# Filler matmuls on TensorE while a norm is computed, in a two-block transformer kernel on one core

## The chip, the cores and the metric

The kernel runs on one core of one Trainium2 chip. The metric is the device time of one execution in microseconds (us); three runs of the kernel before gave 3535.11, 3535.67 and 3539.28 us, median 3535.67. TensorE is PE in the rows (PEld is its loading of stationary operands), VectorE is DVE, ScalarE is ACT, GpSimd is POOL, SyncE is SP.

## The reference, cut to what matters

The input x is 512 tokens by 1024 features. A first block runs twice (l = 0, 1) and a second, hybrid block once. Each part begins with an RMS norm of x along the features:

```
x = x + 0.5*g1 * swiglu(modulate(x, sh1, sc1), ffn1_gate[l], ffn1_up[l], ffn1_down[l])
x = x + g2 * token_mix(modulate(x, sh2, sc2), ...)      # attention branches, gates, output projection
x = x + 0.5*g3 * swiglu(modulate(x, sh3, sc3), ffn2_gate[l], ffn2_up[l], ffn2_down[l])
modulate(x, shift, scale) = x * rsqrt(mean(x*x) + 1e-6) * (1 + scale) + shift
# after both l: rms_norm(x) * final_norm, then the hybrid block:
x = x + merged(rms_norm(x)*norm1_g) @ w_o               # four branches with gates
x = x + square(relu((rms_norm(x)*norm2_g) @ w_up)) @ w_down
```

shift, scale and the gates g come from c_act @ w_ada[l] + b_ada[l]. The next matmuls need the normed x, and the norm needs the whole updated x: at every such border TensorE has to wait.

## The kernel before, in words

x lies in SBUF transposed, as 8 tiles of 128 features x 512 tokens (f32). Weights stream from HBM in one fixed order (`plan()`) through five `raw` buffers. ScalarE rounds each block to fp32r (`wh`), VectorE takes the rest (`wl`), and TensorE multiplies three times per tile pair: `wh*uh + wl*uh + wh*ul` (`three()`, called by `fm()`, L445 to L447). `uh` and `ul` are the two parts of the normed x. Each engine's program is one Python function; they are ordered by semaphores counted in a dry pass. Nothing plans by cost: the order of calls is the order of instructions on each engine.

The stages, with the names used in keys: f10 (first feed-forward, l = 0), m0 (token mix), f20 (second feed-forward), then f11, m1, f21, then "s" (final norm and the hybrid block's first norm), the hybrid block's four branches, and "up" (its feed-forward).

A border works like this (m0 as the example). While the last output tiles are made, GpSimd adds the squares of x tiles 0 to 6 into `acc`; ScalarE squares tile 7 into `tmp1`. TensorE in `norm()` (L498) then does, in order: `sums()` of `acc` (four f32 matmuls with one column of ones, L488), a wait for `tmp1`, `sums()` of `tmp1`, and `row()` (L491 to L496): four f32 matmuls of 128x128, ones times a diagonal that holds 1/rms, which spreads 1/rms over all partitions. Between the sums and the row, VectorE adds the two means (L1471, L1476), GpSimd takes the power -1/2 (L2109) and VectorE builds the diagonal (L1467). After the row, VectorE scales tile k (L1500), ScalarE adds the shift and rounds (L980), VectorE makes `ul` (L1491), for k = 0 to 7. The first two weight blocks after a border are multiplied side by side (`fm_pair()`), six matmuls for each k as it comes.

At the beginning (f10) the squares of x are made by ScalarE and VectorE in `fsq`; TensorE waits for the constants (`CONST`, the tensor `cst` with `ones` and `ident` in it), then does 16 f32 sums (L900 and L901), then the row. The first weights are multiplied in `ffn(first=True)`, L521 to L523.

An f32 matmul stands as two instructions in the trace, and an fp32r one as one ("x8" is four f32 matmuls).

PSUM has eight banks `ps0` to `ps7`. `take(g, b=None)` (L417 to L430) gives a result its bank: the next of a ring when b is None, bank b otherwise. It makes TensorE wait until the bank's last owner was read, if that owner has a reader that frees it:

```
b = ring[0][ring[1] % len(ring[0])]; ring[1] += 1
last = in_bank.get(b); in_bank[b] = g
if last is not None:
    for s in (s_act, s_dve):
        if ("free", last) in s.at: pe.wait_ge(*s["free", last])
```

The ring holds all eight banks in the first block. After each attention its counter is set to 4 (L690). `second()`, the hybrid block, sets it to `[range(6), 0]`: it begins at bank 0 and leaves banks 6 and 7 to the gates; at its end it is set to `[range(8), 0]`. Before `second()`, the sums `("fs", 0)` to `("fs", 2)` and the rows `("r1",)` and `("r", "s")` take the next five banks. VectorE's `apply()` frees the bank of `("r", "s")` with its last tile, `frees=g if k == (0 if after_k else n - 1)` at L1500, since it reads the row out of PSUM for each of the eight tiles.

Of the kernel before, what the change touches and what calls it, by code (L numbers as in the profile page):

```python
# [243 lines left out]
def program(nc, A, OUT):  # L244
# [19 lines left out]
    def sb(ctx, name, shape, dt=F32):  # L264
        return ctx.enter_context(nc.sbuf_tensor(f"s_{name}", shape, dt))

    ps = [top.enter_context(nc.psum_tensor(f"ps{i}", [128, 512], F32)) for i in range(8)]
    cst = sb(top, "cst", [128, ncol])
    x = sb(top, "x", [128, 8, 512])
# [81 lines left out]
    def col(name, i=0, n=1):  # L351
        a, w = cols[name]
        assert i + n <= w
        return cst[:, a + i:a + i + n]

    sA, sB, yh, yl = mq, mk, uh, ul
    ident, ones = col("ident", 0, 128), col("ones", 0, 128)
# [33 lines left out]
    s_x_at = lambda k: (s_x[k // 2], 16)  # L391
# [21 lines left out]
    def tensor_engine(pe, TE):  # L413
# [4 lines left out]
        def take(g, b=None):  # L418
            if b is None:
                b = ring[0][ring[1] % len(ring[0])]  # L420
                ring[1] += 1
            last = in_bank.get(b)
            in_bank[b] = g
            bank_of[g] = b
            if last is not None:
                for s in (s_act, s_dve):
                    if ("free", last) in s.at:
                        pe.wait_ge(*s["free", last])
            return ps[b]
# [56 lines left out]
        def sums(o, at, ap):  # L486
            for b in range(4):
                ins = TE.matmul(o[:, at + b:at + b + 1], ap[:, sl(b)], ones[:, 0:1], start=True, stop=True)  # L488
            return ins

        def row(g, dg):  # L491
            o = take(g)
            for b in range(4):
                pe.wait_ge(*s_dve["diag", g, b])
                ins = TE.matmul(o[:, sl(b)], ones, dg[:, sl(b)], start=True, stop=True)  # L495
            ins.then_inc(*s_pe.up(("ps", g)))  # L496

        def norm(st, parts, dg):  # L498
            for j, (ap, wait) in enumerate(parts):
                o = take(("ms", st, j))  # L500
                pe.wait_ge(*wait)
                sums(o, 0, ap).then_inc(*s_pe.up(("ps", ("ms", st, j))))
            row(("r", st), dg)

        def ffn(st, first=False):
            _, g, u, d, nf = stages[st]
# [35 lines left out]
        def tail(st):  # L542
            return [(acc, s_pool["sq", st]), (tmp[1], s_act["tail", st])]
# [194 lines left out]
        def second():  # L738
# [155 lines left out]
            s_pe.mark(("end", "s"))  # L894
            ring[:] = [list(range(8)), 0]

        pe.wait_ge(*CONST)
        o = take(("ms", "f10", 0))
        for k in range(4):
            pe.wait_ge(*s_dve["sq0 pair", k])  # L900
            ins = sums(o, 4 * k, uf(2 * k + 1))  # L901
        ins.then_inc(*s_pe.up(("ps", ("ms", "f10", 0))))
        row(("r", "f10"), tmp[3])
        for l in range(2):
            if l:
                norm("f11", tail("f11"), tmp[2])
            ffn(f"f1{l}", l == 0)
            norm(f"m{l}", tail(f"m{l}"), tmp[2])
            mix(l)
            norm(f"f2{l}", tail(f"f2{l}"), tmp[2])  # L910
            ffn(f"f2{l}")
        o = take(("fs", 0))
# [4 lines left out]
        o = take(("fs", 1))  # L917
        pe.wait_ge(*s_act["tail", "s"])
        sums(o, 0, tmp[1]).then_inc(*s_pe.up(("ps", ("fs", 1))))
        o = take(("fs", 2))  # L920
# [1375 lines left out]
    for engine in (tensor_engine, scalar_engine, vector_engine, pool_engine, sync_engine):  # L2296
        engine(Waits(), Blank())
# [9 lines left out]
    @block.tensor  # L2307
    def _(e):
        tensor_engine(Waits(e), nc.tensor)
# [170 lines left out]
```

## Time and profile before

| | us |
|---|---|
| three runs, median | 3535.67 |
| three runs, lowest and highest | 3535.11, 3539.28 |
| profiled execution, its own time | 3532.56 |
| its span, first to last instruction | 3530.8 |
| PE busy | 3435.0 |
| mean granted TensorE clock | 0.983 |

The page of the profile gives busy time by engine; the other views used are the waits (who waited for whom), the timeline (start, duration, engine, line, operation, in brackets the idle time before and its releaser), and a table by stretches, which has the granted clock of each. A granted clock of 1.00 is 2.4 GHz, one of 0.50 is 1.2 GHz. In the first 28 us the record of the clock has no entry and shows 1.00; the durations of the matmuls tell it there.

### The profile page before, as it was taken

To read this page: it belongs to the slowest core of one execution; us is meant where nothing else is said; L and a number is where in the kernel's file an instruction comes from. 1 tells how busy PE (TensorE), PEld (TensorE's weight loads), DVE (VectorE), ACT (ScalarE), POOL (GpSimd) and SP (SyncE) were. 2 spreads that over 40 slices of the span, in tenths; PEclk is the share of its full clock that TensorE was granted. 3 is DMA by queue.
4 is the path that set the end of the run, shared out by engine and by line. 5 is a ranking of instruction groups with operands and counts; after the bars stand their busy time and mean duration, and the time that the engine had idled before them with its cause. 6 is when DMAs were issued, how large, how long until landed. Compare 5 with 4: busy or idle time off the path is not lost.

```text
span 3530.8 us, 40839 instructions
## 1 busy us (share of the span) xinstructions
PE 3435.0 (97%) x16646; PEld 2758.3 (78%) x16646; DVE 1786.8 (51%) x3100; ACT 1185.1 (34%) x1990; POOL 287.3 (8%) x238
## 2 busy tenths in 40 slices
PE   8999999999999999999899999999999999999999
PEld 6888786777888788887777878887788777878887
DVE  7666456565565733334654643334453655454433
ACT  3222236542222232223555332223321444223322
POOL 0000220002000200021200100013011000020000
PEclk9999999999999999999999999999999999999999
DMA  6565322123565523223210322322221223122232
GB/s 239 206 211 189 101 78 72 40 69 109 191 219 196 179 98 99 92 95 107 68 49 25 114 83 84 108 82 93 68 78 55 75 73 115 42 96 84 96 107 78
DMA packets 120218, 376.37 MB, mean 107 GB/s; under 512 B 13280, under 2 KB 28000, under 8 KB 120032
## 3 DMA queue, kind: packets, MB, share of 16 engines
q1 hardware_dynamic: 120032, 373.76, 31.8%
q8 instruction: 133, 2.18, 0.3%
q14 instruction: 53, 0.43, 0.0%
HBM read 371.61 MB, written 2.10 MB: 106 GB/s over the span
## 4 chain that ended last, share of the span: by engine, by line
PE 92%; DVE 4%; ACT 2%; issue 1%; POOL 1%; DMA 0%; SPq 0%; POOLq 0%; ACTq 0%; DVEq 0%
PE ps L445 26%; PE ps L446 26%; PE ps L447 26%; PE ps L660 2%; PE ps L683 2%; PE ps L554 2%; PE ps L488 1%; PE ps L495 1%; PE ps L479 1%; PE ps L481 1%; PE ps L480 1%; DVE s_wl L1429 1%; ACT s_wh L944 1%; POOL s_small L2109 0%; PE ps L521 0%
## 5 line engine op out<-in xcount | busy, mean ns | idle before, releaser
L445 PE MATMUL ps<-s_uh,s_wh 128*128 128x512 f32 x2824 | 1137.4, 403 | 30.2 <-DVE s_ul L1491 12.8
L1429 DVE TENSOR_TENSOR s_wl<-s_raw,s_wh 128x1024 fp32r<-128x1024 f32 (+3 forms) x645 | 707.1, 1097 | 845.2 <-ACT s_wh L944 843.0
L446 PE MATMUL ps<-s_uh,s_wl 128*128 128x512 f32 x2824 | 1111.1, 393 | 0.0
L447 PE MATMUL ps<-s_ul,s_wh 128*128 128x512 f32 x2824 | 1110.5, 393 | 0.0
L944 ACT ACTIVATE s_wh<-s_raw 128x1024 fp32r<-128x1024 f32 (+3 forms) x645 | 587.9, 913 | 727.6 <-PE ps L447 531.2
L445 PEld LDWEIGHTS ps<-s_uh,s_wh 128*128 128x128 f32 x2824 | 537.5, 190 | 173.1 <-issue 49.4
L447 PEld LDWEIGHTS ps<-s_ul,s_wh 128*128 128x128 f32 x2824 | 536.6, 190 | 115.1
L446 PEld LDWEIGHTS ps<-s_uh,s_wl 128*128 128x128 f32 x2824 | 537.9, 190 | 109.0 <-issue 2.4
L447 PE MATMUL ps<-s_fl,s_wh 128*128 128x512 f32 x960 | 378.2, 394 | 0.0
L445 PE MATMUL ps<-s_fh,s_wh 128*128 128x512 f32 x960 | 378.2, 394 | 0.0
L446 PE MATMUL ps<-s_fh,s_wl 128*128 128x512 f32 x960 | 378.2, 394 | 0.0
L447 PEld LDWEIGHTS ps<-s_fl,s_wh 128*128 128x128 f32 x960 | 179.5, 187 | 44.5
L446 PEld LDWEIGHTS ps<-s_fh,s_wl 128*128 128x128 f32 x960 | 179.5, 187 | 44.4
L445 PEld LDWEIGHTS ps<-s_fh,s_wh 128*128 128x128 f32 x960 | 179.5, 187 | 44.3
L1011 ACT ACTIVATE s_fh<-s_tmp 128x512 fp32r<-128x512 f32 x120 | 75.8, 632 | 407.3 <-DVE s_tmp L1537 382.4
L1005 ACT ACTIVATE s_tmp<-ps 128x512 f32<-128x512 f32 x120 | 71.7, 597 | 352.8 <-PE ps L447 348.4
L1438 DVE CUSTOM_DVE_ANT_0 s_raw<-s_raw,s_crow 128x1024 f32<-128x1024 f32 x144 | 181.3, 1259 | 0.7 <-DMA s_raw<-w 0.7
L1537 DVE TENSOR_TENSOR s_tmp<-s_tmp,ps 128x512 f32<-128x512 f32 x88 | 60.4, 687 | 178.0 <-PE ps L447 174.2
L2115 POOL TENSOR_TENSOR s_acc<-s_x 128x512 f32<-128x512 f32 x7 | 8.8, 1261 | 1608.1 <-DVE s_x L1519 1544.5
L1463 DVE TENSOR_TENSOR s_fl<-s_tmp,s_fh 128x512 fp32r<-128x512 f32 x120 | 83.1, 692 | 83.8 <-ACT s_fh L1011 83.8
L1519 DVE SCALAR_TENSOR_TENSOR s_x<-ps,s_mod,s_x 128x512 f32<-128x512 f32 x80 | 60.0, 750 | 105.0 <-PE ps L447 105.0
L1128 ACT ACTIVATE s_mT<-ps 128x128 f32<-128x128 f32 (+3 forms) x144 | 57.3, 431 | 145.4 <-PE ps L554 145.4
(401 smaller groups left out, 3374.1 us busy)
## 6 DMA issues: line engine op xcount, KB each, us to landing
s_raw<-w SPq DMA_DIRECT2D x616, 512.0 KB, 3.6
s_raw<-w SPq DMA_DIRECT2D x96, 192.0 KB, 2.4
s_raw<-w SPq DMA_DIRECT2D x64, 256.0 KB, 2.6
s_raw<-w SPq DMA_DIRECT2D x19, 128.0 KB, 2.0
s_x<-x SPq DMA_DIRECT2D x4, 512.0 KB, 6.3
out<-s_x SPq DMA_DIRECT2D x8, 256.0 KB, 2.2
s_raw<-w SPq DMA_DIRECT2D x4, 420.0 KB, 3.6
s_crow<-crow SPq DMA_DIRECT2D x2, 512.0 KB, 3.4
```

What stands on the lines that cost most here:

```text
L445: TE.matmul(o, w_hi(i, k), h, start=first, stop=False)
L446: TE.matmul(o, w_lo(i, k), h, start=False, stop=False)
L447: return TE.matmul(o, w_hi(i, k), l, start=False, stop=last)
L554: ins = TE.transpose(o[:, sl(j)], p[:, sl(j)], ident)
L660: TE.matmul(o[g][:, 0:L], q, k, start=True, stop=True).then_inc(*s_pe.up(("ps", ("S", (st, 2 * t + g)))))
L683: ins = TE.matmul(o[g], v, mT[(n + g) % 4][:, sl(j)], start=kind == "mla" and j == 0, stop=j == i and (kind == "mla" or br == 1))
L944: SC.activation(wh[slot[t]][:, 0:n], raw[t % NRAW][:, 0:n], ACT.Copy).then_inc(*s_hi.up(("hi", t)))
L1005: SC.activation(s[:], bank(("g", st, jj))[:], ACT.Silu if u else ACT.Relu).then_inc(*s_act.up(("gate", st, jj), frees=("g", st, jj)))
L1011: SC.activation(fh[:, j, :], s[:], ACT.Copy).then_inc(*s_act.up(("hh", st, jj)))
L1429: V.tensor_tensor(wl[w][:, 0:n], raw[t % NRAW][:, 0:n], wh[w][:, 0:n].bitcast(F32), SUB).then_inc(*s_lo.up(("lo", t)))
L1438: V.tensor_tensor_reduce(raw[i % NRAW][:], raw[i % NRAW][:], crow[:], 1.0, 0.0, MUL, ADD, mod[:, o:o + 1]).then_inc(*s_dve.up(("raw", i)))
L1463: V.tensor_tensor(dst, src, hi.bitcast(F32), SUB).then_inc(*s_dve.up(key))
```

## The change

A helper `keep_warm(o, n)` writes n f32 products of constants (ones times the first 512 columns of `cst`, 128x512) into a bank that nobody reads. `norm()` now first takes a bank for them, then puts one after the first sums, three after the last sums, and two after the row. It is called at six borders: m0, f20, f11, m1, f21 and up. The "s" border does not go through `norm()` and gets none. At the beginning, a bank is taken, four f32 products of x's tile 0 with itself run as soon as x's first part has landed, and three and two products of constants stand after the sums and after the row. Nothing reads these results; the output does not change.

```diff
+        def keep_warm(o, n):
+            for _ in range(n):
+                TE.matmul(o[:], ones, cst[:, 0:512], start=True, stop=True)
+
         def norm(st, parts, dg):
+            spare = take(("spare", st))
             for j, (ap, wait) in enumerate(parts):
                 o = take(("ms", st, j))
                 pe.wait_ge(*wait)
                 sums(o, 0, ap).then_inc(*s_pe.up(("ps", ("ms", st, j))))
+                keep_warm(spare, 3 if j else 1)
             row(("r", st), dg)
+            keep_warm(spare, 2)
...
+        spare = take(("spare", "f10"))
+        pe.wait_ge(*s_x_at(0))
+        for _ in range(4):
+            TE.matmul(spare[:], x[:, 0, 0:128], x[:, 0, :], start=True, stop=True)
         pe.wait_ge(*CONST)
         o = take(("ms", "f10", 0))
         for k in range(4):
             pe.wait_ge(*s_dve["sq0 pair", k])
             ins = sums(o, 4 * k, uf(2 * k + 1))
         ins.then_inc(*s_pe.up(("ps", ("ms", "f10", 0))))
+        keep_warm(spare, 3)
         row(("r", "f10"), tmp[3])
+        keep_warm(spare, 2)
```

## Rows read from the trace of the kernel before

**Rows 1.** The page, part 1: busy us (share of span) and count.
```profile
PE 3435.0 (97%) x16646; PEld 2758.3 (78%) x16646; DVE 1786.8 (51%) x3100; ACT 1185.1 (34%) x1990; POOL 287.3 (8%) x238
```
**Rows 2.** Waits of TensorE: us in total, times, longest.
```profile
PE ps L445 <- DVE s_ul L1491: 12.8, 5, 2.6
```
**Rows 3.** Stretches: us, each engine's busy time (x), PEclk, DMA share, GB/s.
```profile
393.90:404.00 10.10, 6.80 (x19) 5.58 (x20) 7.93 (x15) 3.74 (x6) 0.28 (x1) 0.50 0.20 76
404.10:412.00 7.90, 7.90 (x36) 6.55 (x35) 4.91 (x7) 2.79 (x4) 1.79 (x5) 1.00 0.20 64
...
1592.00:1598.70 6.70, 4.15 (x14) 3.30 (x13) 5.20 (x9) 2.78 (x4) 0.00 (x0) 0.50 0.17 68
...
2414.60:2424.70 10.10, 6.84 (x23) 5.96 (x24) 7.61 (x22) 2.49 (x5) 1.05 (x1) 0.50 0.00 0
...
3169.00:3175.60 6.60, 4.20 (x11) 3.16 (x11) 6.11 (x10) 3.10 (x5) 0.00 (x0) 0.50 0.01 4
...
535.00:600.00 65.00, 62.48 (x402) 43.48 (x403) 44.68 (x166) 43.58 (x126) 5.97 (x4) 1.00 0.19 65
```
**Rows 4.** Timeline of TensorE at the m0 border.
```profile
391.77 1.02 PE L488 MATMUL ps<-s_cst,s_tmp 128*128 128x1 f32 x8 [1.00 <-ACT s_tmp L985]
394.65 2.04 PE L495 MATMUL ps<-s_tmp,s_cst 128*128 128x128 f32 x8 [1.86 <-DVE s_tmp L1467]
399.25 0.77 PE L445 MATMUL ps<-s_uh,s_wh 128*128 128x512 f32 x1 [2.55 <-DVE s_ul L1491]
```
**Rows 5.** Timeline of VectorE after the m0 border, two steps of k.
```profile
399.02 0.74 DVE L1500 SCALAR_TENSOR_TENSOR s_tmp<-s_x,s_mod,ps 128x512 f32<-128x512 f32 x1
...
400.34 0.74 DVE L1500 SCALAR_TENSOR_TENSOR s_tmp<-s_x,s_mod,ps 128x512 f32<-128x512 f32 x1
```
**Rows 6.** First weight matmul after f20's and f21's borders.
```profile
848.03 0.77 PE L445 MATMUL ps<-s_uh,s_wh 128*128 128x512 f32 x1 [2.55 <-DVE s_ul L1491]
...
2044.01 0.77 PE L445 MATMUL ps<-s_uh,s_wh 128*128 128x512 f32 x1 [2.55 <-DVE s_ul L1491]
```
**Rows 7.** TensorE in the hybrid block: f32 matmuls, rows and sums.
```profile
2529.84 1.02 PE L770 MATMUL ps<-s_lE,s_lv 128*128 128x512 f32 x2
2530.70 1.02 PE L771 MATMUL ps<-s_lE,s_cst 128*128 128x512 f32 x2
...
2727.40 1.05 PE L495 MATMUL ps<-s_tmp,s_cst 128*128 128x128 f32 x8
...
2582.03 3.90 PE L488 MATMUL ps<-s_cst,s_lqk 128*128 128x1 f32 x32
2585.80 0.77 PE L445 MATMUL ps<-s_uh,s_wh 128*128 128x512 f32 x1
```
**Rows 8.** The beginning: VectorE's first operation, TensorE's sums, row, weights.
```profile
5.85 0.69 DVE L2047 TENSOR_TENSOR s_fsq<-s_x 128x512 f32<-128x512 f32 x1 [5.85 <-DMA s_x<-x]
...
11.20 6.99 PE L488 MATMUL ps<-s_cst,s_fsq 128*128 128x1 f32 x32 [11.20 <-DMA s_cst<-cst]
20.07 2.08 PE L495 MATMUL ps<-s_tmp,s_cst 128*128 128x128 f32 x8 [1.88 <-DVE s_tmp L1467]
24.88 0.77 PE L521 MATMUL ps<-s_uh,s_wh 128*128 128x512 f32 x1 [2.73 <-DVE s_ul L1491]
...
28.43 0.50 PE L523 MATMUL ps<-s_ul,s_wh 128*128 128x512 f32 x1
```
**Rows 9.** The up border: VectorE's last update of x, TensorE.
```profile
3163.75 0.69 DVE L1517 TENSOR_TENSOR s_x<-ps,s_x 128x512 f32<-128x512 f32 x1 [2.55 <-PE ps L447]
...
3165.24 1.02 PE L488 MATMUL ps<-s_cst,s_tmp 128*128 128x1 f32 x8 [0.75 <-ACT s_tmp L985]
...
3171.73 0.76 PE L445 MATMUL ps<-s_uh,s_wh 128*128 128x512 f32 x1 [2.40 <-DVE s_ul L1463]
```
**Rows 10.** The s border: TensorE's first weight matmul, VectorE's eighth tile.
```profile
2421.61 0.77 PE L445 MATMUL ps<-s_uh,s_wh 128*128 128x512 f32 x1 [2.40 <-DVE s_ul L1463]
...
2427.69 0.74 DVE L1500 SCALAR_TENSOR_TENSOR s_tmp<-s_x,s_small,ps 128x512 f32<-128x512 f32 x1
```

## The prediction

> **What bounds the kernel now.** I read the page's first part first: TensorE is busy 97% of the span, so only its own work and its few waits can give time [rows 1]. The waits show where those are: among the longest are the first weight matmuls after a border, 2.6 us in each of five, for VectorE's `ul` [rows 2]. The table by stretches then shows what follows such a wait: around each border the clock stands at 1.2 GHz for 6.6 to 10.1 us, and is back at 2.4 GHz, with TensorE busy without a gap, after it [rows 3]. f20, f11 and f21 have the same low stretch as m0 (10.1 to 10.2 us); m1 and up have the shorter ones shown. So the price of a border is the wait plus the work done at half speed at its end. The beginning has the same fault: row and first weights are slow there [rows 8].
>
> **The norm borders, as long as the filler keeps the clock.** At m0 the first weight matmul starts at 399.25 and the clock is low to 404.0 [rows 3, 4]: 4.8 us of weight matmuls at half speed, worth 2.4. Read alike, f20 has 3.2 us, f11 4.9, f21 5.2 (the first and the last of the three starts stand in [rows 6]), m1 2.9, up 3.9. For the five without up that is 21.0 us, worth 10.5. Can the data feed a faster TensorE? VectorE brings one k every 1.32 us [rows 5], and TensorE needs six matmuls for it: 36 in 7.9 us at full clock [rows 3], so about 1.3 to 1.4. It just does, and nothing is late next.
>
> The filler itself: one f32 product of 512 columns takes two instructions, 0.86 us from start to start at full clock (2529.84 to 2530.70) [rows 7], some 1.7 at half. The single one after the first sums fits into the 1.00 us that TensorE waits there [rows 4] (at f20 and f21 the wait is 0.8; cost under 0.1). The three after the last sums do not fit: they take 2.6 us where TensorE waited 1.86 for the diagonal [rows 4]. TensorE runs in order, so the row stands behind them and VectorE behind the row. But the row is then done in 1.05 [rows 7] instead of 2.04 [rows 4]. For m0: sums from 391.77, 0.97 for eight (3.90 for 32) [rows 7], three fillers to 395.3, row to 396.4, against 396.7 before: a gain of 0.3. Worked alike f20 gives 0.4, f11 0.3, f21 0.3, m1 (whose row was only half slow) 0: 1.3 together. The two after the row take 1.7 of a wait of 2.55: nothing; if the clock were low they would take 3.4 and cost 0.9.
>
> Does the filler count as activity? The attention stretch runs at 1.00 for 65 us, most of its matmuls being f32 ones [rows 3]. One-column sums do not: 32 of them in a row end with the clock down, as the next weight matmul lasts 0.77 [rows 7]; the sums at the beginning don't raise it in 7 us either [rows 8]. At a border there is still 0.97 of sums, 0.86 of filler and 0.97 of sums before the long filler begins. I take it that the clock falls there in about one border of five, by the accident of when. Then three fillers stretch by some 1.7 us, but they raise the clock again before the weights, and the border still gains about 0.6. I take 1.5 off for the five: 10.5 + 1.3 - 1.5 = 10.3. The bounds are 11.8 (it never falls) and 5 (it falls under most fillers).
>
> By the Trainium skill ("TensorE: Matmul & The Clock Gate", section "Terms") the penalty is about the throttled time times (1 - K/N). For six low stretches of together 53.7 us it would give 27 us. In this trace the larger part of such a stretch is waiting for VectorE and GpSimd, which the clock does not touch: 4.8 of 10.1 at m0 is weight work.
>
> **The up border.** `spare` takes one more bank of the ring. `second()` ends with its eight `wo` tiles in a ring of six (I counted the takes: tile 6 in bank 0, tile 7 in bank 1), then the ring begins at 0. Before, the first sums took bank 0, long free. Now `spare` takes bank 0 and the first sums bank 1, whose owner is the very last tile. They wait until VectorE has read it: 3163.75 + 0.69, so 3164.5 [rows 9], about 0.9 later. Behind them: sums 0.97, filler 0.86, so the second sums begin at 3166.3 instead of 3165.24; 0.97, fillers 2.6, row 1.05, to 3170.9; plus the 2.40 to the first weight matmul, 3173.3 against 3171.73 [rows 9]. That is 1.6 lost; the clock's half of 3.9 us gives 2.0 back. With the longer pause the clock falls more easily (which would cost about 2.5 more). Between +0.4 and -3; I take -1.4.
>
> **The s border, which has no filler.** This is the largest loss, and it is again the bank. In the f21 to s stretch the ring's counter was 28 at f21's norm and 91 at `("fs", 0)`: banks 3, 4, 5, 6, and 7 for `("r", "s")`. With f21's `spare` all move by one, and `("r", "s")` takes bank 0. `second()` restarts the ring at 0, so its first weight product takes bank 0 and must wait until the row is freed. VectorE frees it with its eighth tile, at 2427.69 + 0.74 = 2428.4 [rows 10], where TensorE began at 2421.61. Every matmul of the hybrid block is queued behind. VectorE's tiles don't wait for TensorE, so no deadlock, only a wait of 6.9 us. The clock is low before and after this and needs about as long to rise from the new start, so I add nothing for it (bounds: 1 either way). Nothing is gained back: TensorE bounds what follows. Bounds 5.9 and 7.9; 0 if I have miscounted.
>
> **The beginning.** Four products of x start at 5.85, when x's first part is there [rows 8]. At half clock they would take 6.8 us and end at 12.7. The weights' own rise took 3.6 us from the first matmul (24.88 to 28.43), so the clock should rise at 9 to 12 and the four end between 11.3 and 12.7; the sums could start at 11.2. The 32 sum instructions take 3.9 instead of 6.99 [rows 7, 8]: end at 15.2 to 16.6 instead of 18.2. Then 2.6 of filler instead of 1.88 of wait, and a row of 1.05 instead of 2.08: the row is done 1.5 to 3 earlier, and 3.6 us of weight work at half speed give 1.8 more. But 3.9 us of sums is just the length in which the clock fell in the hybrid block [rows 7]. If it falls, the fillers take up to 5.1 us and most of the gain is gone. Between 0.9 and 4.2, I take 2.4. It is kept, as VectorE's weight splits shift with the row.
>
> **Sum.** 10.3 (five borders) + 2.4 (beginning) - 1.4 (up) - 6.9 (s) = 4.4 us. From the profiled span, 3530.8, that gives 3526.4, and 3528.2 for that execution's own time of 3532.56. The three runs' median is 3.1 above that execution; I keep the distance: 3535.67 - 4.4 = 3531.3 us. By bounds (11.8, 4.2, 0.4, -5.9) the best is 10.5 us, the worst (5, 0.9, -3, -7.9) a loss of 5.0.
>
> **Rivals.**
> - The wait for the bank does not come, or is hidden. For it: the code is long and a count by hand can be wrong. Against: the ring's counter is plain arithmetic. Then 4.4 + 6.9 = 11.3 gained: 3524.4. Chance 12%. The rule of the page, in which whole low stretches count, would give 27 + 2.4 - 1.6 - 6.9, some 21 gained: 3515; 1%.
> - The fillers come too late and the clock falls under them at nearly every border. For it: only 0.86 of 2.8 us before them is work that counts. Against: attention holds it with gaps. Then the worst sum: 3540.7. Chance 16%.
> - Products of constants don't hold the clock at all (slower). They run slow themselves: three take 5.1 where 1.86 was free (3.3 us), two take 3.4 where 2.55 was (0.9), 4.2 at each of six borders; at the beginning 1.5 + 4.2; and s: 25 + 6 + 7 = 38 lost, 3573. It decides when the clock is low at the end of the second sums and stays so. Against: the f32 matmuls in attention [rows 3]. Chance 6%.
> - TensorE, started earlier, meets late weights: the blocks behind the first two are split by VectorE after its eighth tile. TensorE would wait for `wl` and lose half of the borders' gain: 3536. Against: the first two blocks last 11 us and VectorE needs 11 for its eight tiles and is then free [rows 5]. Chance 7%.
>
> The forecast itself has 58%, its own range 3527.5 to 3536.
>
> **How the numbers follow.** The range reaches from the first rival to the second: 3524 to 3541. What a measurement can tell is 0.2%, 7.1 us: faster means below 3528.6. The forecast lies 2.7 above that; I give it a quarter of its 58%. With the first rival that is 0.27 for faster. Slower (above 3542.7) is the third rival and a little of the second, 0.09. The rest, 0.64, is no change that can be told.
>
> **What would show it.** At m0, f20, f11, m1, f21: granted clock 1.00 through the border, first weight matmul within 0.4 us of its old distance from the last weight matmul, 0.39 us long. Rows of about 1.05 us that start directly behind the third filler, VectorE idle for them. At s: TensorE idle about 9 us before its first weight matmul, released by VectorE's L1500. At up: first sums released by L1517. At the beginning: sums 0.12 us each. It is wrong if the s wait is 2.4 us as before, or if the fillers stand 0.86 us apart per instruction instead of 0.43.

## The result and the profile after

The changed kernel ran 20 times beside 20 runs of the kernel before: medians 3532.15 and 3537.88 us, ratio 0.9978 with the 95% interval 0.9971 to 0.9986, that is 7.8 us (5.0 to 10.3) faster. The medians alone lie 5.7 us apart; the ratio is an estimate of its own and need not equal theirs. A second set on another occasion (after_again, below) gave 0.9987 (0.9978 to 0.9996), 4.6 us, with medians again 5.7 us apart. Forecast were 4.4 us and 3531.3 us. Two executions of the changed kernel were in a slow state and are left out of the ratios: 3683.23 us at a mean granted clock of 0.893 in the first set, 5802.31 us at 0.579 in the second.

The profiled execution is one of the slower of the 20: 3536.48 us, span 3534.6, longer than the span before. So no single trace gives the gain; the stages do. First the page, its first part and its most used new line (the last from the view of one line):

```profile
span 3534.6 us, 41018 instructions
PE 3460.7 (98%) x16736; PEld 2759.4 (78%) x16736; DVE 1787.6 (51%) x3100; ACT 1185.0 (34%) x1990; POOL 288.3 (8%) x238
...
L500 PE MATMUL ps<-s_cst x82: 592/592/1201, 16.5 to 3176.1; 128*128 128x512 f32 x82
```

PE is busy 26 us more than in [rows 1]: 41 fillers of constants as 82 instructions, and four of x. Busy time went up and the median time down. (Behind the change the line numbers are higher: L1500 of before is L1513, L1491 is L1504, L521 is L528.)

The waits of TensorE after (us in total, times, longest):

```profile
PE ps L445 <- DVE s_tmp L1513: 9.4, 1, 9.4
...
PE ps L445 <- DVE s_ul L1504: 4.2, 5, 0.8
PE ps L495 <- DVE s_tmp L1480: 3.9, 2, 2.4
```

The second line answers to [rows 2]: five waits of 2.6 have become 0.8, the rest is filler. The third is what is left of the waits for the diagonals, those without filler. The first is new: a single wait of 9.4 us.

The m0 border after, TensorE's timeline (against [rows 4]):

```profile
388.79 0.95 PE L488 MATMUL ps<-s_cst,s_acc 128*128 128x1 f32 x8
389.60 1.10 PE L500 MATMUL ps<-s_cst 128*128 128x512 f32 x2
390.74 1.02 PE L488 MATMUL ps<-s_cst,s_tmp 128*128 128x1 f32 x8
391.62 2.82 PE L500 MATMUL ps<-s_cst 128*128 128x512 f32 x6
394.28 1.05 PE L495 MATMUL ps<-s_tmp,s_cst 128*128 128x128 f32 x8
395.17 1.88 PE L500 MATMUL ps<-s_cst 128*128 128x512 f32 x4
397.89 0.47 PE L445 MATMUL ps<-s_uh,s_wh 128*128 128x512 f32 x1 [0.84 <-DVE s_ul L1504]
```

From the first sums to the first weight matmul it takes 9.10 us. The row begins straight behind the third filler and takes 1.05 us, not 2.04. The first weight matmul is a fast one, 0.47. The table by stretches after shows the clock of this border, of the next weights, and of the s border (against [rows 3]):

```profile
388.90:398.00 9.10, 8.23 (x38) 4.72 (x37) 4.64 (x12) 1.96 (x3) 1.02 (x1) 1.00 0.50 174
398.10:408.00 9.90, 9.90 (x45) 8.15 (x45) 9.55 (x14) 5.30 (x7) 1.38 (x5) 1.00 0.01 2
...
3168.70:3177.40 8.70, 8.02 (x36) 4.83 (x37) 3.44 (x10) 1.72 (x3) 1.02 (x1) 1.00 0.00 0
2404.60:2422.90 18.30, 6.64 (x30) 6.29 (x30) 12.04 (x32) 4.39 (x9) 2.07 (x2) 0.50 0.04 16
2423.00:2428.20 5.20, 5.20 (x12) 4.09 (x13) 2.46 (x4) 2.05 (x3) 0.00 (x0) 0.50 0.08 13
```

In the last two rows lies the price: at the s border TensorE is at 1.2 GHz for more than 23 us, and idle for 9.4 of them in one wait, 11.7 in all. Its timeline there, and VectorE's eighth tile (against [rows 10]):

```profile
2409.88 3.75 PE L495 MATMUL ps<-s_tmp,s_cst 128*128 128x128 f32 x16 [2.39 <-DVE s_tmp L1480]
2422.99 0.76 PE L445 MATMUL ps<-s_uh,s_wh 128*128 128x512 f32 x1 [9.36 <-DVE s_tmp L1513]
```
```profile
2422.11 0.73 DVE L1513 SCALAR_TENSOR_TENSOR s_tmp<-s_x,s_small,ps 128x512 f32<-128x512 f32 x1
```

The first weight matmul starts 0.15 us after that tile's end, as said ahead. The beginning after (against [rows 8]):

```profile
6.03 6.47 PE L907 MATMUL ps<-s_x 128*128 128x512 f32 x8 [6.03 <-DMA s_x<-x]
12.33 4.34 PE L488 MATMUL ps<-s_cst,s_fsq 128*128 128x1 f32 x32
16.53 5.47 PE L500 MATMUL ps<-s_cst 128*128 128x512 f32 x6
21.79 1.10 PE L495 MATMUL ps<-s_tmp,s_cst 128*128 128x128 f32 x8
22.73 1.88 PE L500 MATMUL ps<-s_cst 128*128 128x512 f32 x4
25.62 0.47 PE L528 MATMUL ps<-s_uh,s_wh 128*128 128x512 f32 x1 [1.01 <-DVE s_ul L1504]
```

The three fillers (six instructions) after the sums take 5.47 us, twice what three take at the m0 border: the clock had fallen within the sums and came back while they ran, so that the row is fast but late. This is not so in every execution. In no_shift_again (below), with the same instructions here, the clock held and the row began at 18.16:

```profile
15.50 2.82 PE L500 MATMUL ps<-s_cst 128*128 128x512 f32 x6
18.16 1.05 PE L495 MATMUL ps<-s_tmp,s_cst 128*128 128x128 f32 x8
```

Of seven traces with this beginning (after, after_again, no_shift, no_shift_again, two_fill, no_first, s_fill) the row began between 21.2 and 21.8 us in five, at 18.96 in s_fill and at 18.16 in no_shift_again.

The up border after (against [rows 9]) has a wait of 0.83 us ahead of its first sums, which is the shifted bank, and a fast first weight matmul:

```profile
3168.65 1.02 PE L488 MATMUL ps<-s_cst,s_acc 128*128 128x1 f32 x8 [0.83 <-DVE s_x L1530]
3169.53 1.10 PE L500 MATMUL ps<-s_cst 128*128 128x512 f32 x2
...
3177.40 0.47 PE L445 MATMUL ps<-s_uh,s_wh 128*128 128x512 f32 x1 [0.68 <-DVE s_ul L1476]
```

Where the stages begin tells more than the span. Each number is the time from one border's first sums (L488 on `s_acc`) to the next one's, worked out from the timelines; "start" goes up to the m0 border, "hybrid" from the s to the up border, and "up" from the up border to the end of the span.

| us | start | m0 | f20 | f11 | m1 | f21 | hybrid | up |
|---|---|---|---|---|---|---|---|---|
| before | 389.8 | 448.8 | 373.6 | 374.5 | 448.1 | 374.4 | 754.4 | 367.2 |
| after | 388.8 | 447.8 | 372.1 | 371.8 | 450.1 | 371.6 | 766.5 | 365.9 |
| after_again | 388.4 | 450.6 | 371.6 | 371.8 | 447.8 | 371.6 | 762.3 | 366.0 |
| banks_only | 391.1 | 447.8 | 374.4 | 373.1 | 449.4 | 373.0 | 765.1 | 366.5 |
| no_shift | 388.3 | 447.4 | 371.5 | 371.7 | 451.1 | 371.6 | 754.2 | 365.9 |
| no_shift_again | 385.2 | 449.1 | 371.6 | 371.7 | 447.4 | 371.5 | 755.7 | 365.9 |
| all_three | 385.5 | 448.9 | 370.9 | 371.0 | 448.9 | 370.9 | 752.4 | 365.3 |

Against the trace of before, f20, f11 and f21 win 1.5 to 2.9 us in every trace with three fillers, and 2.7 to 3.5 in all_three's with two. One trace of before is a thin base for this: in banks_only, whose borders have no filler either, f11 and f21 take 1.4 us less than in before. There the low stretch lasts 6.8 us instead of 10.2 (from 1218.5 and 2041.2). So the gain of a single border depends on how the slow stretch happened to fall; measured at each border, from the first sums to the first weight matmul and with half of the low time behind it, the five gain 12.3 us together against before and 11.8 against banks_only. m0 and m1, with an attention each, scatter by 3 us between traces of one kernel.

The hybrid block takes 8 to 12 us more in the three traces whose banks are shifted, and not in the other rows. But its total alone doesn't prove the bank: among the traces that are not in the table, all with unshifted banks, it takes 751.6 us in all_three_again, 757 to 760 in no_start, one_column, two_fill, no_first and more_fill, and 770.7 in s_fill, whose clock is low for long in another part of the block (last section). What tells the bank is the wait of 9.36 us and its releaser.

### The profile page after: what moved, and what is told of

The parts are those of the page before. It is cut to its first block, busy times and chain, and to the rows that moved or that the text cites. A ratio compares the mean times of both kernels' runs of the same rounds, so it can differ in the third digit from the quotient of the medians.

```text
span 3534.6 us, 41018 instructions
## 1 busy us (share of the span) xinstructions
PE 3460.7 (98%) x16736; PEld 2759.4 (78%) x16736; DVE 1787.6 (51%) x3100; ACT 1185.0 (34%) x1990; POOL 288.3 (8%) x238
## 4 chain that ended last, share of the span: by engine, by line
PE 92%; DVE 4%; ACT 2%; issue 1%; DMA 0%; POOL 0%; SPq 0%; ACTq 0%; POOLq 0%; DVEq 0%
PE ps L445 26%; PE ps L447 25%; PE ps L446 25%; PE ps L667 2%; PE ps L690 2%; PE ps L561 2%; PE ps L488 1%; PE ps L479 1%; PE ps L481 1%; PE ps L480 1%; PE ps L495 1%; DVE s_wl L1442 1%; PE ps L500 1%; ACT s_wh L957 0%; PE ps L528 0%
```

## The experiments

All were timed in five rounds beside the kernel before, with 5 to 12 executions of each; "faster" is (1 - ratio) times the median before, with its interval.

**banks_only.** The kernel before with the takes of the change and none of its matmuls:

```diff
         def norm(st, parts, dg):
+            take(("spare", st))
...
+        take(("spare", "f10"))
         pe.wait_ge(*CONST)
```

> The kernel before, with only the seven bank takes of the change and none of its fillers. Bank theory: the first weight matmul of the hybrid block waits for VectorE's eighth tile (released by the scaling of x, not by ul), some 7 us later than before, and the up border's first sums wait 0.9 us of which 0.25 shows: 7.2 us slower than before, ratio 1.0020. Rival (the wait at that border belongs to the fillers or to the clock, not to the bank): no difference, ratio 1.000.

Measured: ratio 1.0030 (1.0018 to 1.0041), 10.6 us slower (6.4 to 14.5). Its timeline at the s border:

```profile
2428.12 0.77 PE L445 MATMUL ps<-s_uh,s_wh 128*128 128x512 f32 x1 [9.36 <-DVE s_tmp L1502]
```

The same wait as in the changed kernel, to 0.01 us, without a filler. The bank theory stands, the rival falls. The middle of the interval is above the 7.2 reckoned. In its trace the wait gives 7.0; the first weights are then slow until some 5.6 us after their start, where before it was 3.1, which is 1.2 more; 0.8 goes in front of the first sums at up. Some 1.7 of the hybrid block's 10.7 remain, about what other stretches of the table scatter by. The up stage then gives 0.7 back (366.5 against 367.2). The reckoned 7.2 us lie within the interval, so that the whole costs more than that is not shown by the ratio.

**no_shift.** The changed kernel with the fillers' bank beside the ring:

```diff
-            spare = take(("spare", st))
+            spare = take(("spare", st), ring[0][(ring[1] + 4) % 8])
...
-        spare = take(("spare", "f10"))
+        spare = take(("spare", "f10"), ring[0][(ring[1] + 4) % 8])
```

> The changed kernel, with the fillers' bank taken four places ahead in the ring and the ring's counter left alone, so that all other results have their old banks. Bank theory: the changed kernel's gain of 7.8 us plus the 6.9 us of the s border and some 1 us at the up border: 15.5 us faster than before, ratio 0.9956; TensorE idle 2.4 us before the hybrid block's first weight matmul, released by ul. Rival (TensorE would have waited there for other things): like the changed kernel, 0.9978.

Measured: 0.9964 (0.9950 to 0.9978), 12.7 us faster. The s border in its trace:

```profile
2413.98 0.77 PE L445 MATMUL ps<-s_uh,s_wh 128*128 128x512 f32 x1 [2.40 <-DVE s_ul L1476]
```

The wait is back at 2.40 us, released by `ul`, and the hybrid block takes 754.2 us, as before. By the ratio alone the two theories (0.9956, 0.9978) were not told apart, since the interval holds both; the trace tells them apart. To settle the size, both kernels ran once more on one chip.

**after_again and no_shift_again.** The same two kernels, unchanged.

> The changed kernel, on the same chip as no_shift_again, so that the two can be set against each other: 0.9978 of the time before, as in its first 20 runs. In its first trace the hybrid block took 11.3 us longer than before, in banks_only 10.8, where I had reckoned 6.9 + 0.25; if that was accident of where the clock fell, this trace shows 7 to 9.

> The same kernel as no_shift. Bank theory: 7 to 11 us faster than after_again, ratio to before 0.995 to 0.996; rival (the bank costs the changed kernel less, since its lost time overlaps other waits): under 4 us faster, 0.997.

Measured: 0.9987 (0.9978 to 0.9996) and 0.9957 (0.9945 to 0.9969). The intervals don't overlap: without the shift it is 0.30%, 10.6 us, faster. after_again's hybrid block took 762.3 us, 7.9 more than before, within the 7 to 9 expected. The first trace of the same kernel took 4.2 us more: its sums before the two rows were already slow, so that the rows began 1.4 us later, and the low stretch at 2520.4 lasted 10.2 us instead of 3.4. (Counted as in the table, the 11.3 and 10.8 of the expectation are 12.1 and 10.7.) The changed kernel itself came out at 4.6 us here, 0.9987 where 0.9978 was expected.

**one_column.** no_shift, with fillers that occupy TensorE but have one column:

```diff
         def keep_warm(o, n):
-            for _ in range(n):
-                TE.matmul(o[:], ones, cst[:, 0:512], start=True, stop=True)
+            for _ in range(3 * n + n // 2):
+                TE.matmul(o[:, 0:1], ones, cst[:, 0:1], start=True, stop=True)
```

> As no_shift, but each filler of 512 columns is replaced by three or four products of one column, which take TensorE about as long at full clock (0.12 us an instruction); the four products of x at the beginning stay. Clock theory: they occupy TensorE without keeping its clock, so it falls at every border as before, the one-column products double in length, the row stands behind them: 1.5 to 2 us lost at each of six borders and the start, 12 us slower than before, ratio 1.0035. Rival (the gain comes from order or timing, not from the clock): as no_shift, 0.9956.

Measured: 1.0028 (1.0018 to 1.0038), 9.9 us slower. The m0 border in its timeline, and the table by stretches:

```profile
394.19 2.37 PE L500 MATMUL ps<-s_cst 128*128 128x1 f32 x20
396.42 1.83 PE L495 MATMUL ps<-s_tmp,s_cst 128*128 128x128 f32 x8
398.05 2.98 PE L500 MATMUL ps<-s_cst 128*128 128x1 f32 x14
```
```profile
391.40:396.60 5.20, 4.96 (x44) 4.85 (x43) 2.33 (x8) 0.63 (x1) 1.02 (x1) 1.00 0.70 227
396.80:406.80 10.00, 10.00 (x35) 8.74 (x35) 8.29 (x13) 4.39 (x7) 0.00 (x0) 0.50 0.09 34
```

TensorE is busy 4.96 of 5.20 us and the clock falls all the same, for the same 10 us as before the change. It fell at all six borders of this trace, where in no_shift it fell at none. So the gain does not come from TensorE being occupied, nor from order or timing: all of these are nearly as in no_shift. What differs is that the fillers have 512 columns there and one here. This pair of kernels differs by 22.6 us.

**no_start.** no_shift without the three groups of the beginning:

```diff
-        pe.wait_ge(*s_x_at(0))
-        for _ in range(4):
-            TE.matmul(spare[:], x[:, 0, 0:128], x[:, 0, :], start=True, stop=True)
...
-        keep_warm(spare, 3)
         row(("r", "f10"), tmp[3])
-        keep_warm(spare, 2)
```

> As no_shift, without all fillers of the beginning (the four products of x, the three and the two). The changed kernel's trace shows its first weight border 1.0 us earlier than before, while my forecast for the beginning was 2.4 us. If 1.0 is typical: 14.5 us faster than before (ratio 0.9959); if 2.4 is: 13.1 (0.9963). Rival (the beginning's fillers cost more than they bring): faster than no_shift.

Measured: 0.9977 (0.9968 to 0.9987), 8.1 us faster than before, so 4.6 us behind no_shift, and the intervals overlap. By the traces "start" was 389.8, 391.1 and 390.6 in three traces without the fillers (before, banks_only, no_start) and 388.8, 388.4, 388.3 and 385.2 in four with them: 2.8 us by the means. With the three other traces that have them (two_fill 388.1, no_first 388.3, s_fill 386.2) it is 2.9. The beginning's fillers pay: the two groups of traces don't overlap. Trace against trace the gain is 1.0 to 3.0 us where the clock fell in the sums, and 4.6 to 5.9 in no_shift_again, where it held; so 1.0 is the low end, and the mean stays open between 2.4 and 4.6.

**two_fill.** no_shift with one filler less before the row:

```diff
-                keep_warm(spare, 3 if j else 1)
+                keep_warm(spare, 2 if j else 1)
```

> As no_shift, with two fillers instead of three after the last sums of each norm. Three (2.66 us to the row in the changed kernel's trace) overrun the 1.86 us that the diagonal takes; two take 1.77. My theory: the row starts 0.7 us earlier at six borders, the clock still holds: 4 us faster than no_shift, 17 us faster than before, ratio 0.9952. Rival (the third filler is needed, the clock falls at some borders): as no_shift or slower, 0.9964 to 0.998, with granted clock 0.50 at some of the six borders.

Measured: 0.9950 (0.9932 to 0.9969). The m0 border in its timeline:

```profile
390.91 1.96 PE L500 MATMUL ps<-s_cst 128*128 128x512 f32 x4
392.82 1.16 PE L495 MATMUL ps<-s_tmp,s_cst 128*128 128x128 f32 x8
```

From the end of the sums to the row's start it is now VectorE's time, and the clock held at all six. f20, f11 and f21 each take 0.6 to 0.7 us less than in no_shift (370.9, 371.1, 370.9). The total, a gain 5 us above no_shift's first figure, is not clear of it; the stages are. The profiled execution hides them, since its hybrid block took 760.4 us (last section).

**no_first.** no_shift without the filler between the two sums:

```diff
-                keep_warm(spare, 3 if j else 1)
+                keep_warm(spare, 3 if j else 0)
```

> As no_shift, without the filler between the two sums of a norm. Theory that it is needed (it divides about 3 us in which only sums run): the clock falls under the three fillers at most borders, 1.7 us each, some 6 us slower than no_shift, ratio 0.998. Rival (the three long ones alone hold it): as no_shift, 0.9964.

Measured: 0.9967 (0.9957 to 0.9978), beside the rival's 0.9964; the theory's 0.998 lies outside. In its trace the clock fell at one border of six, m1:

```profile
1581.54 0.95 PE L488 MATMUL ps<-s_cst,s_acc 128*128 128x1 f32 x8
1583.39 1.55 PE L488 MATMUL ps<-s_cst,s_tmp 128*128 128x1 f32 x8 [0.91 <-ACT s_tmp L998]
1584.81 5.47 PE L500 MATMUL ps<-s_cst 128*128 128x512 f32 x6
1590.07 1.31 PE L495 MATMUL ps<-s_tmp,s_cst 128*128 128x128 f32 x8
...
1593.93 0.47 PE L445 MATMUL ps<-s_uh,s_wh 128*128 128x512 f32 x1 [0.84 <-DVE s_ul L1504]
```

There the three fillers take 5.3 us to the row instead of 2.7 and the weights start 3.3 us late, though fast. The theory's "at most borders" was wrong. The filler may be an insurance: without it the clock fell once in six borders, with it at none of the 60 in the other ten traces with fillers of 512 columns. One fall is too few to show it.

**s_fill.** no_shift with fillers at the s border:

```diff
+        spare = take(("spare", "s"), ring[0][(ring[1] + 5) % 8])
         o = take(("fs", 0))
...
+        keep_warm(spare, 1)
         o = take(("fs", 1))
...
+        keep_warm(spare, 2)
         row(("r1",), tmp[2])
         row(("r", "s"), tmp[0])
+        keep_warm(spare, 2)
```

> As no_shift, with fillers at the s border too, which the change leaves out: one after the first sums, two before and two after its two rows. There the clock is low for 10 us in no_shift. The two rows should take 1.9 instead of 3.75 us and some 3 to 5 us of weight work run at full clock: 1.8 + 2 = 4 us faster than no_shift, ratio 0.9953. Rival (the 16 sums and two rows let the clock fall in spite of them): as no_shift.

Measured: 0.9952 (0.9935 to 0.9969). Its profiled execution is its slowest run, for a reason of its own (last section), and the clock fell at its s border in spite of the fillers (low from 2405.5 for 6.8 us). There the fillers ran slow, and the first weight matmul came 13.8 us after the first sums, against 12.4 in no_shift, though the weights were then fast: about nothing won. On the ratio it is where expected, but the interval also holds no_shift's.

**all_three.** two_fill and s_fill, and the beginning rearranged:

```diff
             ins = sums(o, 4 * k, uf(2 * k + 1))
+            if k == 1:
+                keep_warm(spare, 1)
...
-        keep_warm(spare, 3)
+        keep_warm(spare, 2)
         row(("r", "f10"), tmp[3])
```

> two_fill and s_fill together, and at the beginning one filler in the middle of the sums and two instead of three after them. In the changed kernel's trace the clock rises there only near the end of the four products of x, falls again in the sums, and the three fillers take 5.3 us instead of 2.6, so the row starts 1.7 us later than before. With the sums divided: row 2 to 3 us earlier than in no_shift. Sum: 4 + 4 + 2.5, 10.5 us faster than no_shift, 23 us faster than before, ratio 0.9934. Rival (the clock falls anyway in the beginning): 21 us, 0.9941.

Measured: 0.9938 (0.9922 to 0.9954), 21.9 us faster than before. Its beginning, by the timeline:

```profile
11.36 1.95 PE L488 MATMUL ps<-s_cst,s_fsq 128*128 128x1 f32 x16 [0.20 <-DMA s_cst<-cst]
13.17 1.10 PE L500 MATMUL ps<-s_cst 128*128 128x512 f32 x2
...
17.84 1.16 PE L495 MATMUL ps<-s_tmp,s_cst 128*128 128x128 f32 x8
```

The row starts at 17.84, where the changed kernel had 21.79 and the one before 20.07. (In no_shift_again it started at 18.16 without the division, so that part of the 4 us is where the clock happened to fall.) This time the clock also held at the s border (1.00 from 2396.2 to 2407.8), with the first weight matmul 11.7 us after the first sums. The ratio doesn't tell the forecast from its rival: 0.9934 and 0.9941 both lie in the interval.

**all_three_again and more_fill.** The same kernel, and one with fillers in the token mixes and in the hybrid block's sums:

```diff
             sums(o, 0, acc)
+            keep_warm(spare, 1)
...
                 if h == 2:
+                    keep_warm(take(("spare3", st), ring[0][(ring[1] + 4) % 8]), 3)
                     row(("rk", st), acc)
...
                 ins = sums(o, 4 * i, xsq[:, i, :])
+                if i in (2, 5):
+                    keep_warm(spare, 1)
```

> The same kernel as all_three, as the base of more_fill: 0.9938.

> As all_three, with fillers at three more places where its trace has a low clock: one after the first inner sums of each token mix, three before the row of the mix's second inner norm (TensorE waits 2.95 us there before), two within the 64 sums of the hybrid block's second branch. Theory: the low stretches at 486, 517, 1681, 1711 and 2698 us (3.4 us, the last 13.7) go: 1.7 us each for four, 5 for the last: 10 us faster than all_three, ratio 0.991. Rival (the fillers overrun their waits, or the clock falls elsewhere instead): as all_three, 0.9938.

Measured: 0.9939 (0.9925 to 0.9952), a repeat, and 0.9933 (0.9921 to 0.9945). The rival holds: no difference that can be told. In more_fill's trace m0 and m1 are 445 us long, 1 to 4 shorter than in the two traces of all_three, but the hybrid block takes 757.7 instead of 752.4: among the 64 sums two fillers don't hold the clock (it is low from 2680.0 for 13.7 us) and cost their own time. At its s border, where its fillers are those of all_three, the clock fell for 3.4 us (from 2393.3); so of four traces with fillers there it held in two, both of all_three. In all_three_again the clock fell at the beginning (the two fillers took 3.36 us, and the row began at 18.67). More_fill does not beat all_three, which is the simpler one and the version to keep, 0.6% below the kernel before.

## Why the prediction was right, point by point

- **Fillers hold the clock at the norm borders: right.** f20, f11 and f21 won 1.5 to 2.1, 2.7 to 2.8 and 2.8 to 2.9 us; my steps gave 2.0, 2.8 and 2.9. That the three agree one by one owes something to luck, since the gains are counted against the very trace that the steps were read from: with banks_only as the base they would be 2.3 to 2.9, 1.3 to 1.4 and 1.4 to 1.5. The sum of the five borders, 12.3 or 11.8 by the two bases, stands against my 11.8. The three terms (half the slow weight work, the late row, the fast row) each appear in the timeline: at m0 the row starts 0.7 us later after the first sums than before (5.49 against 4.83), takes 1.05 instead of 2.04, and ends 0.3 earlier; the weights are fast.
- **"The clock falls in about one border of five": wrong.** It fell at none of the 30 norm borders in five traces with all of the norm's fillers (after, no_shift, no_start, and the two repeats). The 1.5 us that I took off were not lost. The rival of fillers that come too late is out, and with it the one of constants that don't count. The rival of late weights is out too: behind each of the five borders TensorE is busy without a gap for 29 to 30 us. Behind m0:

```profile
398.10:428.00 29.90, 29.90 (x133) 24.72 (x133) 16.78 (x21) 12.54 (x16) 1.79 (x5) 1.00 0.28 89
```

- **m0 and m1: not to be seen in one trace.** The attention stretches scatter by 3 us for accidents of the clock elsewhere; in after_again it is low for 6.8 us from 550.2, where the first trace has nothing, and m0 is 2.8 us longer. The borders themselves show 9.10 us from first sums to first fast weight, and weights at full clock behind it: 2.8 us won at m0 and 1.5 at m1, which the stage's total hides.
- **The s border: right in place and size.** 9.36 against 2.40 us is 6.96, forecast 6.9, and released by the eighth scaling. The whole shift of banks may cost more than I counted: 10.6 us (6.4 to 14.5) in banks_only and 10.6 between the repeats, but only 4.9 between the first figures of after and no_shift. The reckoned 7.2 is within the scatter of these. In banks_only's trace the slow stretch behind the wait was longer and cost 1.2 us more (I had set this to nothing, bound 1); in after_again's it lasted 3.0 us, as before, so this too goes by accident.
- **The up border: the wait was right (0.83 us, forecast 0.9), the sum too dark.** First weights came 1.4 us later, measured from where the sums could start; the clock held, so 2.0 came back: +0.5, and I had taken -1.4.
- **The beginning: within its bounds.** In the profiled execution the clock did fall in the sums, the fillers took 5.3 us to the row, and the row came 1.7 us later than before; but the row and all weights were fast. In one trace of seven, no_shift_again's, it did not fall. 2.8 by the traces against 2.4.
- **Sum.** 4.4 forecast; 7.8 (5.0 to 10.3) and 4.6 (1.4 to 7.8) measured. The forecast misses the first interval by 0.6 us. The two terms that were too dark (1.5 and 1.9 us) make up the 3.4 us between 4.4 and 7.8; what the bank cost beyond 6.9 works against them. With the terms as the traces give them the sum is 12.3 + 2.8 + 0.5 - 7.0 = 8.6. So the mechanisms were right, and the size was 3.4 us low against the first set and 0.2 against the second. That 3531.3 us lies so close to the measured median, 3532.15, is luck: the kernel before had a median of 3537.88 in the same set, 2.2 us above the 3535.67 from which the forecast was taken. The rival in which whole low stretches count (some 21 us) is out, as is the one in which the bank costs nothing (11.3): the wait is there.

## What to carry to other kernels

Look at the clock after every wait of TensorE, not only at the wait: the slow work behind it can cost as much, and products of constants with 512 columns, sized to fit inside the wait, won it back here; products of one column did not. Give the scratch bank of such fillers a place outside the ring: here one more turn of the ring cost 5 to 11 us of the 13 to 15 that the fillers brought. Before adding any allocation to a rotating pool, follow the rotation to every point where it is reset or where a bank is held long.

## What the runs showed of the hardware that was not expected

The clock can stay low although TensorE is never idle. In s_fill's profiled run the fourth branch of the hybrid block ran at 1.2 GHz for 36.6 us with TensorE busy throughout; by stretches:

```profile
3000.00:3022.00 22.00, 21.94 (x152) 17.19 (x150) 11.79 (x23) 3.10 (x4) 0.00 (x0) 1.00 0.21 73
3023.40:3060.00 36.60, 36.60 (x128) 29.45 (x127) 3.67 (x6) 5.04 (x8) 3.28 (x4) 0.50 0.02 8
```

The work there is made of small matmuls (52 of 64x64, 24 of 64x128, 24 of 128x128) with 28 weight matmuls of 512 columns between; this execution took 3540 us, where the kernel's median is 3522, and its hybrid block 770.7. In two_fill's trace the clock is low for 27 us in the same part of that branch; in the other twelve traces for 7 to 10. Executions of one kernel differ by up to 24 us (s_fill, 3516.07 to 3540.16), more than the changed kernel gains. In the traces the longer ones have more low clock here or in the attention stretches; the executions without a trace can't be told. What decides it was not tried.
